# Behind the attentions of a three-mixer transformer kernel: turned heads between the matmuls of the first output panels

## The reference

```
f1 = swiglu(rmsnorm(h, g[0]), ffn_w_gate[i, 0], ffn_w_up[i, 0], ffn_w_down[i, 0])
h = h + FFN_RES * rmsnorm(f1, g[1])
hn = rmsnorm(h, g[2])
m = neighborhood_attention(hn, ...) or diff_attention(hn, ...)      # both end in  o @ w_o
h = h + rmsnorm(m, g[3])
f2 = swiglu(rmsnorm(h, g[4]), ...)
h = h + FFN_RES * rmsnorm(f2, g[5])
```

## Time and profile before

| what | value |
|---|---|
| median of 3 runs | 1523.96 us (1520.89 to 1527.64) |
| the profiled execution | 1518.83 us, span 1517.0 us |
| busy share of the span | PE 96%, DVE 63%, ACT 43%, POOL 4% |
| chain that ended last | PE 79%, DVE 10%, issue 4%, ACT 3%, DMA 2% |
| granted clock of TensorE | 0.99 in the mean |
| weight splits: `w_lo` of 2048 columns, `w_hi` of 2048 columns | 2.28 us on DVE, 1.91 us on ACT |

### The profile page before, as it was taken

The page is one execution under the profiler, slowest core; times in us unless marked ns, Lnnn a source line. Parts: engine busy times, 40 slices in busy tenths (PEclk is TensorE's granted clock), DMA queues, the critical chain, the costliest instruction groups (busy, mean ns, idle before and its releaser), DMA issues.

```text
span 1517.0 us, 27189 instructions
## 1 busy us (share of the span) xinstructions
PE 1460.0 (96%) x11458; PEld 1404.6 (93%) x11458; DVE 955.2 (63%) x1229; ACT 659.0 (43%) x856; POOL 53.2 (4%) x75
## 2 busy tenths in 40 slices
PE   6999999999999999999999998999999998999998
PEld 5999999978999999999999977899999996999997
DVE  5665567457766646665547566766646657877644
ACT  4444345445544335434335345553434533444432
POOL 0000010011000000000010000100001010100000
PEclk9999999999999999999999999999999999999998
DMA  5555884512455665654464510465555640355551
GB/s 179 171 188 166 224 238 148 175 35 84 140 167 180 177 191 153 195 185 153 149 192 149 170 54 29 141 193 183 173 162 161 197 137 1 112 179 182 193 188 63
DMA packets 250779, 233.52 MB, mean 154 GB/s; under 512 B 29759, under 2 KB 249844, under 8 KB 250688
## 3 DMA queue, kind: packets, MB, share of 16 engines
q1 hardware_dynamic: 250224, 231.96, 49.4%
q10 hardware_dynamic: 464, 0.25, 0.1%
HBM read 230.99 MB, written 1.12 MB: 153 GB/s over the span
## 4 chain that ended last, share of the span: by engine, by line
PE 79%; DVE 10%; issue 4%; ACT 3%; DMA 2%; POOL 1%; SPq 0%; DVEq 0%; ACTq 0%
PE acc L582 23%; PE acc L583 23%; PE acc L584 23%; DVE h L1553 2%; PE aux L747 1%; DVE h L1547 1%; ACT w_hi L1125 1%; DVE rstd L1518 1%; DVE x_lo L1524 1%; PE acc L889 1%; PE acc L919 1%; PE aux L869 1%; PE aux L910 1%; DMA raw<-in_ffn_w_up 1%; DVE h L1608 1%
## 5 line engine op out<-in xcount | busy, mean ns | idle before, releaser
L582 PE MATMUL acc<-x_hi,w_hi 128*128 128x272 f32 (+1 forms) x2096 | 599.2, 286 | 10.5 <-DVE z L1639 6.2
L583 PE MATMUL acc<-x_lo,w_hi 128*128 128x272 f32 (+1 forms) x2096 | 599.9, 286 | 0.0
L584 PE MATMUL acc<-x_hi,w_lo 128*128 128x272 f32 (+1 forms) x2096 | 597.9, 285 | 0.0
L1513 DVE TENSOR_TENSOR w_lo<-raw,w_hi 128x2048 fp32r<-128x2048 f32 (+1 forms) x230 | 483.9, 2113 | 88.5 <-ACT w_hi L1125 88.0
L1125 ACT ACTIVATE w_hi<-raw 128x2048 fp32r<-128x2048 f32 (+3 forms) x251 | 406.6, 1627 | 138.2 <-DMA raw<-in_ffn_w_down 49.6
L582 PEld LDWEIGHTS acc<-x_hi,w_hi 128*128 128x128 f32 x2096 | 396.8, 189 | 12.6 <-issue 10.1
L583 PEld LDWEIGHTS acc<-x_lo,w_hi 128*128 128x128 f32 x2096 | 395.6, 189 | 0.1
L584 PEld LDWEIGHTS acc<-x_hi,w_lo 128*128 128x128 f32 x2096 | 395.6, 189 | 0.0
L582 PE MATMUL acc<-hid_hi,w_hi 128*128 128x272 f32 (+1 forms) x704 | 204.5, 290 | 6.5 <-DVE w_lo L1513 6.5
L583 PE MATMUL acc<-hid_lo,w_hi 128*128 128x272 f32 (+1 forms) x704 | 203.0, 288 | 0.0
L584 PE MATMUL acc<-hid_hi,w_lo 128*128 128x272 f32 (+1 forms) x704 | 201.9, 287 | 0.0
(11 more groups left out here) (295 smaller groups left out, 1621.6 us busy)
## 6 DMA issues: line engine op xcount, KB each, us to landing
raw<-in_ffn_w_gate SPq DMA_DIRECT2D x44, 1024.0 KB, 5.3
raw<-in_ffn_w_up SPq DMA_DIRECT2D x44, 1024.0 KB, 5.3
raw<-in_ffn_w_down SPq DMA_DIRECT2D x32, 768.0 KB, 4.5
raw<-in_ffn_w_down SPq DMA_DIRECT2D x32, 640.0 KB, 4.3
raw<-in_w_up SPq DMA_DIRECT2D x16, 1024.0 KB, 5.3
raw<-in_w_down SPq DMA_DIRECT2D x16, 1024.0 KB, 5.0
raw<-in_na_w_qkv SPq DMA_DIRECT2D x12, 1024.0 KB, 5.2
raw<-in_da_w_qkv SPq DMA_DIRECT2D x12, 1024.0 KB, 5.2
```

The lines of the kernel that those rows point to most:

```text
L582: nc.tensor.matmul(o, wh, xh, start=first, stop=False)
L583: nc.tensor.matmul(o, wh, xl, start=False, stop=False)
L584: return nc.tensor.matmul(o, wl, xh, start=False, stop=last)
L1513: nc.vector.tensor_tensor(w_lo[:, slot, w], raw[:, slot, w], w_hi[:, slot, w].bitcast(F32), ALU.subtract)\
```

## The change

In all three mixers the turning of the heads goes into `from_heads`. Chunk `c` is turned and then chunk `c - 2` is multiplied for panels 0 and 1, so that the two panels end together. The product of one chunk is the body of `first_panels`, now `shared_chunk`. Panel 2 goes to `aux[:, 0:2]`, the banks of turned chunks. Panel 0 and 1 fill all of `acc`, so the first turn of the neighborhood block waits for all evictions of its attention. `sum_rest`, whose first matmuls write `aux[:, 0]`, waits until panel 2 is evicted.

The splits move: that of output panel 1 from behind the attention into step (2, 3) of the projections, on DVE ahead of that step's eviction; that of panel 2 from output step 0 to directly behind the heads' splits.

```diff
-            if n % 2 == 0 and n > 0 and isinstance(i, int) and (i, j) == (0, 2):
+            shared = n > 0 if n % 2 == 0 else n // 2 in (NA, DA, MIX)
+            if shared and isinstance(i, int) and (i, j) == (0, 2):
                 return aux[:, 0:2, :]
...
                 for k in range(DC):
-                    pe.wait_ge(x_hi_ready, SPLIT_IN[k_] + k + 1)
+                    shared_chunk(n, SPLIT_IN[k_], tokens, k)
+
+            def shared_chunk(n, base, tokens, k):
+
+                    ph = PHASES[n]
+                    pe.wait_ge(x_hi_ready, base + k + 1)
                     for j in range(2):
...
-                    pe.wait_ge(x_ready, SPLIT_IN[k_] + k + 1)
+                    pe.wait_ge(x_ready, base + k + 1)
...
-            def from_heads(k_, tokens):
+            def from_heads(k_, tokens, meta):
...
-                ready = ready_heads(k_)
-                for j in range(3):
-                    panel(n, 0, j, ph.a0 + j - 1, acc[:, j % 2, :, :], range(8), True, True, x_hi[:, :, 0:tokens],
-                          x_lo[:, :, 0:tokens], ready if j == 0 else lambda k: None)
+                if k_ != NA:
+                    keep_warm(aux[:, 1, :], 10 if k_ == DA else 7)
+                for c in range(8 + 2):
+                    if c < 8:
+                        turn_heads(k_, c, meta)
+                    if c >= 2:
+                        shared_chunk(n, SPLIT_HEADS[k_], tokens, c - 2)
+                panel(n, 0, 2, None, banks(n, 0, 2), range(8), True, True, x_hi[:, :, 0:tokens], x_lo[:, :, 0:tokens],
+                      lambda k: None)
                 last_panel(k_, ph.a0 + 2, range(8), True, x_hi[:, :, 0:tokens], x_lo[:, :, 0:tokens])
...
             def sum_rest(k_, tokens):
 
+                pe.wait_ge(acc_free, PHASES[2 * k_ + 1].a0 + 3)
                 keep_warm(aux[:, 0, :], 2)
...
-                    if k == NA and c % 4 == 0:
-                        pe.wait_ge(s["evicted"], 2 + c // 2)
...
+                if k == NA and c % 4 == 0:
+                    pe.wait_ge(s["evicted"], 4)
...
# ACT, output_steps (DVE's has the same with low)
-                    if local <= last - 2:
+                    if local <= last - 2 and (groups_of > 1 or local > 0):
                         high(n, i, j + 2)
...
# ACT, projections
-                        if (i, j) != (2, 3) and (i, j) not in ((0, 0), (0, 1)):
+                        if (i, j) not in ((0, 0), (0, 1)):
                             high(n, i, j + 2)
...
-                        high(n, 2, 5)
...
+                    high(n + 1, 0, 2)
...
# DVE, projections
+                        if (i, j) == (2, 3):
+                            split(n, i, j)
                         evacuate(n, i, j, tokens, dst, p, SCALE if queries else None)
...
-                    low(n, 2, 5)
+                    low(n + 1, 0, 2)
```

More of the change, by code:

```diff
@@ L647, in first_panels @@
                             mm.then_inc(panel_used, 1)
-            def ready_heads(k_):
-                def ready(k):
-                    pe.wait_ge(x_ready, SPLIT_HEADS[k_] + k + 1)
-                return ready
             def from_x(k_, tokens, before_panel=None):
@@ L934, in da_attention, with turn_heads @@
                             .then_inc(s["turned"], 1)
-            def turn_heads(k, meta):
+            def turn_heads(k, c, meta):
                 s = mixers[k]
                 base = SPLIT_HEADS[k]
-                if k != NA:
-                    keep_warm(aux[:, 1, :], 10 if k == DA else 7)
-                for c in range(8):
-                    if k == NA and c % 4 == 0:
-                        pe.wait_ge(s["evicted"], 2 + c // 2)
-                        if c == 0:
-                            pe.wait_ge(meta_copied, 2)
-                    if k == DA:
-                        pe.wait_ge(s["o_step"], c + 1)
-                    if k == MIX and c == 0:
-                        pe.wait_ge(s["evicted"], 2)
-                    if k == MIX and c == 4:
-                        pe.wait_ge(ml_norm, 7)
-                    wait(pe, x_ready, base + c - 3 if c >= 4 else 0)
-                    for t in range(2):
-                        tr = nc.tensor.transpose(aux[:, c % 4, P * t:P * t + P], o_rows[:, t, P * c:P * c + P], ident[:, :])
-                    if meta:
-                        tr = nc.tensor.transpose(aux[:, c % 4, NX:NT], o_meta[:, P * c:P * c + P], ident[0:NM, 0:NM])
-                    tr.then_inc(s["o_turned"], 1)
+                if k == NA and c % 4 == 0:
+                    pe.wait_ge(s["evicted"], 4)
+                    if c == 0:
+                        pe.wait_ge(meta_copied, 2)
+                if k == DA:
+                    pe.wait_ge(s["o_step"], c + 1)
+                if k == MIX and c == 0:
+                    pe.wait_ge(s["evicted"], 2)
+                if k == MIX and c == 4:
+                    pe.wait_ge(ml_norm, 7)
+                wait(pe, x_ready, base + c - 3 if c >= 4 else 0)
+                for t in range(2):
+                    tr = nc.tensor.transpose(aux[:, c % 4, P * t:P * t + P], o_rows[:, t, P * c:P * c + P], ident[:, :])
+                if meta:
+                    tr = nc.tensor.transpose(aux[:, c % 4, NX:NT], o_meta[:, P * c:P * c + P], ident[0:NM, 0:NM])
+                tr.then_inc(s["o_turned"], 1)
             pe.wait_ge(in_full, 16 * 5)
@@ L1089, in _ @@
                     attention(k, rope_part)
-                    turn_heads(k, False)
                 if k in (NA, DA, MIX):
-                    from_heads(k, tokens_out)
+                    from_heads(k, tokens_out, k == NA)
                 elif k == MLP:
@@ L1251, in step @@
                         bias = [gains[:, b:b + 1] for b in range(G_NA_BO + 2 * g, G_NA_BO + 2 * g + 2)] if k == NA else None
-                        square(2 * k + 1, g, acc[:, g % 2, :, 0:tokens], tokens, bias)
-                    if local <= last - 2:
+                        square(2 * k + 1, g, banks(n, 0, g)[:, :, 0:tokens] if groups_of == 1 else acc[:, g % 2, :, 0:tokens], tokens, bias)
+                    if local <= last - 2 and (groups_of > 1 or local > 0):
                         high(n, i, j + 2)
@@ L1673, in step @@
                         for m in range(2):
-                            ins = scaled_y(k, 2 * g + m, acc[:, g % 2, m, 0:tokens], tokens)
+                            ins = scaled_y(k, 2 * g + m, (banks(n, 0, g) if groups_of == 1 else acc[:, g % 2, :, :])[:, m, 0:tokens], tokens)
                         ins.then_inc(acc_free, 1)
-                    if local <= last - 2:
+                    if local <= last - 2 and (groups_of > 1 or local > 0):
                         low(n, i, j + 2)
```

4 lines of the change are left out of this document (removed).

## The result

| kernel | median | over the kernel before |
|---|---|---|
| before (6 runs) | 1520.82 us | |
| changed (6 runs) | 1536.32 us (1533.81 to 1538.89) | +15.5, ratio 1.0096 [1.0078, 1.0115] |

The forecast was 1536.9 us, with a range of 1527 to 1543: slower, as predicted. The profiled execution took 1538.89 us (span 1537.1, mean granted clock 0.981) and was the longest of the six, so the two traces differ by 20.1 us of span where the medians differ by 15.5.

The account below looks back on a forecast made before the run. TensorE, busy nearly the whole span, was taken as the bound. Neighborhood 7.2, differential 1.5 and hybrid 4.15 us made 12.9, added to the median of the runs shown: 1536.9 us, range 1527 to 1543.

Parts of the forecast that it names:

- Fronts: First turned head to end of output panel 1: differential 2.6 us earlier, hybrid 1.35 earlier, neighborhood 1.7 later.
- the switches between turns and products: TensorE's cost of alternating turning and multiplying in the fronts: taken as 0, at most 6 us in all.
- the 1.7: Neighborhood front: the first turn waits for all evictions of the attention, so panel 1 ends 1.7 us later.
- Tails: End of panel 1 to end of last panel: longer by 5.5 us (neighborhood), 4.1 (differential), 4.2 (hybrid).
- DVE's chain behind the last `x_lo`: Tails: reciprocal, `h` products, evictions and splits queue in order; differential block's TensorE waits 2.7 us before the last panel.
- the middle taken: Tails: second of two weight loads issued together lands between +5.4 and +10.8 us; 8.1 taken.
- POOL's 1.30 + 0.73 come on top of DVE's chain: Tails: POOL's additions of squares wait out DVE's splits, adding 2.05 us before the last sum.
- cost hides in the wait for the sum: Tails: a clock fall after the wait ahead of the last panel would add nothing, TensorE waiting for the sum anyway.
- the moved split of the hybrid block: Hybrid projections: DVE's panel 1 split ahead of the eviction makes the column turns start 1.3 us later.
- rival 2: TensorE's clock also falls behind the tails' waits, up to 1.5 us a block: 17 in all, 1541; chance 0.15.
- has idle time overall: Argument for the not-slower rival: DVE's burst fits and turning is hidden, -5.2 us in all, 1518.8; chance 0.1.

Follow-up runs that it names:

- early_late: Changed kernel with DVE's reciprocal and `h` products between the `x_lo` pieces and the last split behind panel 2's eviction: 1533.00 us, +12.3 over the kernel before.
- warm_na: Changed kernel with 12 filler matmuls of TensorE ahead of the neighborhood block's first turn: 1538.85 us, +18.1 over the kernel before.
- mix_evac: Changed kernel with the eviction ahead of the moved split in the hybrid block's last projection step: 1531.16 us, +10.4 over the kernel before.
- small_add: Changed kernel with POOL's additions of panel 2's squares and of the two halves cut to 16 columns: 1536.18 us, +15.7 over the kernel before.
- dve_sum: Kernel with both DVE-order edits, plus additions of squares on DVE instead of POOL and next block's splits behind them: 1524.07 us, +3.6 over the kernel before.
- The three single blocks: Kernel before with the whole change in one block alone: neighborhood 1528.52 us, differential 1522.41 us, hybrid 1530.27 us.
- mix_split_only: Kernel before with only the hybrid block's split of output panel 1 moved into the last projection step, ahead of the eviction: 1528.19 us, +7.3.
- mix_split_warm: Kernel before with the hybrid block's split moved and 12 more filler matmuls ahead of the column turns: 1523.93 us, 3.2 over the kernel before.

## Why the prediction was right, and where it wasn't

- **Fronts.** Differential: -2.4 for -2.6 (from the attention's last matmuls; the first turn itself came 0.4 later), hybrid -1.6 for -1.35; so the switches between turns and products cost next to nothing, as taken. Neighborhood: the 1.7 was right as work; in the profiled execution the clock added as much again.
- **Tails.** The mechanism held in all three blocks: DVE's chain behind the last `x_lo` makes the last panel wait (3.39, 2.31, 2.06), and early_late takes that wait away by moving DVE's reciprocal and products (it also moves a split of DVE and ACT that stands behind the one awaited). The loads issued together fit the middle taken: in early_late the second was used 8.0 behind its issue (951.35 to 959.37); warm_na had 9.2. The tails are 0.5 to 0.9 shorter than forecast.
- **The step that doesn't hold as a price** is "POOL's 1.30 + 0.73 come on top of DVE's chain". It is right as a description: POOL's sum ends 1.95 behind the last split (971.32 against 969.37), and where the clock stayed up TensorE waited 1.80 for it (mix_evac). But beside the fall of the clock it costs only 0.4 to 0.7 a block (small_add), not 2. I had called that fall a thing whose "cost hides in the wait for the sum". It does, and as much hides the other way round: the two lie side by side, and either alone makes the tail 16.5 to 18.5 us. Only when both went (dve_sum) was it 13.3 to 14.4.
- **The mis-sized term** is the moved split of the hybrid block: 1.3 forecast, 7.3 measured. Its delay was right (1.24). Behind the wait that it opens, 1.16 us ahead of an attention of small matmuls, the clock was down for 13 to 17 us in each of the seven profiles that have it. I had looked for the clock behind long waits in dense work only (rival 2) and given it at most 1.5 a block.
- **The total** came out within 1 us of the median because errors cancel. By the rows the pieces at full clock cost 10.9 instead of 12.9, and 4 to 5 come on top that were not in the sum, most of it clock as far as the traces tell. The forecast was also built on a median of three runs, 1523.96, which is 3.1 above that of all six, 1520.82: as a difference, 12.9 was forecast and 15.5 measured. The forecast of "slower" rested on the right mechanism; that its number fits so closely is luck.

What stays open: whether the fall of the clock in the neighborhood block's front is tied to its wait (seen in 2 of 6 profiles with that wait), and what brings the clock down in the hybrid attention where no wait stands ahead of it. The three single blocks sum to 18.5 when the whole change costs 15.5; at equal clock they sum to 7.5 against 8.3, so that this difference is one of the clock between runs.

## What to carry to other kernels

When work is moved under an engine that "has idle time overall", write down its queue from the moved piece on: an in-order engine gives idle time only where nothing behind the piece is awaited. Where a wait for two engines is repaired, expect it to come back at the next engine until both are gone; here the repair of DVE's queue alone brought 3 us, that of both 12. And a wait of a microsecond in front of a sparse stretch of TensorE can cost five times its length: bring the eviction forward (5 us here) or fill the wait (4 us here, with fillers that reached 1.5 us too far; a filling that fits exactly was not run). When a cost is priced, ask what stands beside it: here POOL's sum and the fall of the clock each hid the other, and taking away one alone brought less than 1 us a block.

## What the runs showed of the hardware

- Behind a wait of 1.16 us ahead of the hybrid attention the granted clock fell to 0.50 for 13 us (mix_split_only), and not at all with that wait filled, though the work began later (mix_split_warm). A long fall came in all 7 profiles with the wait and in 3 of 7 without it.
- Behind waits of 2.1 to 3.4 us ahead of a last panel the clock fell for 3 to 4 us in 14 of 15 cases. Behind waits of 1.89 and 2.68 us at the sum it stayed at 1.00 (early_late), behind one of 2.82 us it fell: the length of a wait alone doesn't decide.
- A GpSimd addition that starts beside a DVE split gets nowhere until the split ends, whatever its size: one of 32 columns took 2.20 us and ended with the split, one of 512 columns took 2.91 us and ended 1.1 us behind it, and took 1.30 us undisturbed. The Trainium skill (SBUF — State Buffer, Who interferes with whom) says so of the loser of the shared read interface, and the trace agrees; the same addition of 512 columns on DVE took 0.69.
- The mean granted clock of the same kernel differs between executions from 0.981 to 0.992, and the time goes with it at 1.2 us for 0.001.
